# Sampled sparse attention of a decode step on one core: the order of squares, roots, score reads, top-k and tails

## The reference, cut to what matters

```
s_c = einsum('blghd,bcgd->bghlc', qg, kc) * scale + bias_c     # scores of the 64 compressed blocks
p_c = masked_softmax(s_c, dist_c >= 0);  o_cmp = p_c @ vc
ps = sum over heads of p_c, pairs of blocks added              # 32 blocks of 64 keys, and the block of the new ones
score = where(forced, 1e4, ps);  top_val, top_idx = top_k(score, 16)
ks = rms_norm(rows[:, :, 2], g_k[1])                           # every cached key is normalised
o_sel = masked_softmax(q @ ks[top blocks] * scale + bias) @ vs[top blocks]
kw = rms_norm(win_k, g_k[2]);  o_win = softmax over the window @ win_v
o = gate0 * o_cmp + gate1 * o_sel + gate2 * o_win
```

## Time and profile before

| | us |
|---|---|
| median of 3 runs | 3475.95 (3474.07 to 3480.38) |
| the profiled execution: its time | 3476.59 |
| the profiled execution: its span | 3474.7 |
| PE busy | 3191.6 (92%) |
| DVE busy | 1594.4 (46%) |
| ACT busy | 1274.2 (37%) |
| POOL busy | 204.1 (6%) |
| sampled sparse attention (from 811 to 1054 us of the span) | 243 |
| PE busy in it | 153.0 |

### The profile page before, as it was taken

How to read it: one execution, slowest core, us unless ns; L and a number is a source line. 1 busy time by engine, 2 the same in 40 slices (tenths; PEclk the granted TensorE clock), 3 DMA queues, 4 the chain that set the end, 5 groups by cost and what they waited for, 6 DMA issues and landing times. The chain is left out here.

```text
span 3474.7 us, 56585 instructions
## 1 busy us (share of the span) xinstructions
PE 3191.6 (92%) x23855; PEld 2983.6 (86%) x23855; DVE 1594.4 (46%) x1672; ACT 1274.2 (37%) x1312; POOL 204.1 (6%) x137
## 2 busy tenths in 40 slices
PE   7899999875669999999999999967789999999999
PEld 6799999753338999999999999945389999999999
DVE  5543444345554544334443354355755443344433
ACT  5432344334553434323333342235034343233332
POOL 0000000012330000000000000025200000000000
PEclk9999999978889999999999999977799999999999
DMA  6555454414554445455555545303644554555553
GB/s 217 155 166 176 140 165 127 158 49 134 183 170 165 150 158 169 159 169 167 162 169 164 166 147 167 121 33 105 242 133 144 167 167 161 169 163 164 169 161 134
DMA packets 317268, 537.10 MB, mean 155 GB/s; under 512 B 18245, under 2 KB 115519, under 8 KB 316104
## 3 DMA queue, kind: packets, MB, share of 16 engines
q1 hardware_dynamic: 316440, 529.73, 47.3%
q10 hardware_dynamic: 624, 4.46, 0.3%
HBM read 517.23 MB, written 25.19 MB: 156 GB/s over the span
## 5 line engine op out<-in xcount | busy, mean ns | idle before, releaser
L509 DVE TENSOR_TENSOR project_weights_low<-ring,project_weights_high 128x2048 fp32r<-128x2048 f32 x344 | 788.4, 2292 | 1207.1 <-ACT project_weights_high L441 1207.1
L441 ACT ACTIVATE project_weights_high<-ring 128x2048 fp32r<-128x2048 f32 x344 | 658.7, 1915 | 1256.7 <-PE project_banks L369 1256.6
L367 PE MATMUL project_banks<-high,project_weights_high 128*128 128x288 f32 x2560 | 762.0, 298 | 31.2 <-DVE project_weights_low L499 27.3
L368 PE MATMUL project_banks<-low,project_weights_high 128*128 128x288 f32 x2560 | 760.4, 297 | 0.0
L369 PE MATMUL project_banks<-high,project_weights_low 128*128 128x288 f32 x2560 | 760.1, 297 | 0.0
L367 PE MATMUL project_banks<-up_high,project_weights_high 128*128 128x288 f32 x2048 | 605.7, 296 | 0.0
L368 PE MATMUL project_banks<-up_low,project_weights_high 128*128 128x288 f32 x2048 | 605.5, 296 | 0.0
L369 PE MATMUL project_banks<-up_high,project_weights_low 128*128 128x288 f32 x2048 | 605.3, 296 | 0.0
L367 PEld LDWEIGHTS project_banks<-high,project_weights_high 128*128 128x128 f32 x2560 | 487.1, 190 | 32.9 <-DVE project_weights_low L499 28.1
L368 PEld LDWEIGHTS project_banks<-low,project_weights_high 128*128 128x128 f32 x2560 | 486.7, 190 | 0.0
L369 PEld LDWEIGHTS project_banks<-high,project_weights_low 128*128 128x128 f32 x2560 | 485.5, 190 | 0.0
(11 more groups left out here) (516 smaller groups left out, 3033.3 us busy)
## 6 DMA issues: line engine op xcount, KB each, us to landing
ring<-in_w_up_dram SPq DMA_DIRECT2D x128, 1024.0 KB, 5.3
ring<-in_w_down_dram SPq DMA_DIRECT2D x128, 1024.0 KB, 5.1
ring<-in_gla_w_in_dram SPq DMA_DIRECT2D x40, 1024.0 KB, 5.1
h<-in_cache_nsa_kv_dram SPq DMA_DIRECT2D x256, 128.0 KB, 2.3
ring<-in_w_out_dram SPq DMA_DIRECT2D x32, 1024.0 KB, 5.2
ring<-in_nsa_w_in_dram SPq DMA_DIRECT2D x28, 1024.0 KB, 5.1
sp_keys_values<-in_cache_nsa_kv_dram SPq DMA_DIRECT2D x80, 256.0 KB, 3.8
ring<-in_w_mem_kv_dram SPq DMA_DIRECT2D x16, 1024.0 KB, 5.3
```

What stands on the lines that cost most here:

```text
L367: nc.tensor.matmul(bank, w_high, moving_high[:, kt], start=(kt == 0), stop=False)
L368: nc.tensor.matmul(bank, w_high, moving_low[:, kt], start=False, stop=False)
L441: nc.scalar.activation(weights_high[:, c % 2], g.ring[:, c % RING], ACT.Copy).then_inc(rounded, 1)
L509: nc.vector.tensor_tensor(weights_low[:, c % 2], g.ring[:, c % RING], weights_high[:, c % 2].bitcast(F32), ALU.subtract).then_inc(split, 1)
```

## The change

The change gives other places to the same instructions. On ACT, a tick is now `square(k+2)`, `root(k+1)`, `copy_keys(k)`. On DVE, `sum_squares(k+2)` comes ahead of `take_scores`, which moves from even to odd ticks. The top-k is cut by pair: pair 0's stays in the front, those of pairs 1, 2 and 3 go to ticks 3.5, 5.5 and 7.5, each with its own bias instructions (three small ones for each pair in place of three for all). Tails move by one tick for the sets and the output, and by half a tick for DVE's scaling. The front of ACT and PE moves as well: ACT's exponential goes behind `square(0)`, PE's group sum behind `turn_keys(0)`.

```
 tensor:  front   yield -0.5 -> 0.5;  yield 1.5 -> 2.5
          tails   tail(t, 2) -> 3;  2.4 + 0.4 * i -> 3.4 + 0.4 * i;  tail(t, 5) -> 6
 scalar:  tails   2 + 0.4 * i -> 3 + 0.4 * i   (copy_set);  tail(t, 1.2) of the exponential stays
 vector:  front   yield 0.1 -> 0.6
          tails   tail(t, 1.6) -> 2.1;  4.9 -> 5.9;  5.5 -> 6.5   (tail(t, 1.1) stays)
@@ scalar
             def front():
+                yield -1.5
                 act.wait_ge(cmp_shifted, 1)
                 nc.scalar.activation(s_cmp[:], s_cmp[:], ACT.Exp).then_inc(cmp_exped, 1)
-                yield 1.5
+                yield 2.5
...
                     yield k
+                    if in_range(k + 2):
+                        square(k + 2)
                     if in_range(k + 1):
                         root(k + 1)
                     if in_range(k):
                         copy_keys(k)
-                    if in_range(k + 2):
-                        square(k + 2)
@@ vector
                 for t in range(PAIRS):
+                    if t:
+                        yield 2 * t + 1.5
                     for r in range(TOP_ROUNDS):
...
-                linked(nc.vector.tensor_scalar(unselected[:], block_score[:], 0.0, MASKED, ALU.is_ge, ALU.mult))
...
+                    linked(nc.vector.tensor_scalar(unselected[:, t], block_score[:, t], 0.0, MASKED, ALU.is_ge,
+                                                   ALU.mult))
+                    linked(nc.vector.tensor_scalar(sel_bias[:, t], unselected[:, t], far, None, ALU.add))
...
                         invert(k + 1)
-                    if k % 2 == 0 and in_range(k - 1):
-                        take_scores((k - 2) // 2)
                     if in_range(k + 2):
                         sum_squares(k + 2)
+                    if k % 2 and in_range(k - 2):
+                        take_scores((k - 3) // 2)
```

More of the change, by code:

```diff
@@ L1950, in front @@
                 mm.then_inc(small_scored, 1)
-                yield -0.5
+                yield 0.5
                 pe.wait_ge(cmp_ready, 1)
@@ L2028, in tails @@
                 for t in range(PAIRS):
-                    yield tail(t, 2)
+                    yield tail(t, 3)
                     pe.wait_ge(scaled, t + 1)
@@ L2033, in tails @@
                     for i in range(SETS):
-                        yield tail(t, 2.4 + 0.4 * i)
+                        yield tail(t, 3.4 + 0.4 * i)
                         multiply_set(t, i)
@@ L2037, in tails @@
                             turn_set(t, i + 2)
-                    yield tail(t, 5)
+                    yield tail(t, 6)
                     pe.wait_ge(o_taken, t + 1)
@@ L2104, in tails @@
                     for i in range(SETS):
-                        yield tail(t, 2 + 0.4 * i)
+                        yield tail(t, 3 + 0.4 * i)
                         copy_set(t, i)
@@ L2164, in front @@
                 linked(nc.vector.memset(block_score[:, :, half - 1:half + 1], FORCED))
+                near = g.bias_near[:, 0:P].rearrange("p (n k) -> p n k", k=SEL_LEN)
                 for t in range(PAIRS):
+                    if t:
+                        yield 2 * t + 1.5
                     for r in range(TOP_ROUNDS):
@@ L2171, in front @@
                         linked(nc.vector.match_replace(block_score[:, t], top[:, r], block_score[:, t], MASKED))
[L2173 to L2179, removed]
+                    linked(nc.vector.tensor_scalar(unselected[:, t], block_score[:, t], 0.0, MASKED, ALU.is_ge,
+                                                   ALU.mult))
+                    linked(nc.vector.tensor_scalar(sel_bias[:, t], unselected[:, t], far, None, ALU.add))
+                    linked(nc.vector.tensor_tensor(
+                        near_bias[:, t].rearrange("p (n k) -> p n k", k=SEL_LEN), near,
+                        unselected[:, t, half - 2:half].unsqueeze(2).to_broadcast([P, 2, SEL_LEN]), ALU.add))
             def sum_squares(n):
@@ L2237, in tails @@
                                             ).then_inc(negated, 1)
-                    yield tail(t, 1.6)
+                    yield tail(t, 2.1)
                     dve.wait_ge(exped, t * 2 + 2)
```

17 lines of the change are left out of this document (8 added, 9 removed).

## The result

The changed kernel takes 3471.14 us in the median (20 runs, 3465.36 to 3476.07), the kernel before 3478.14 in the same session (20 runs). The ratio is 0.9979, 95% interval 0.9973 to 0.9985: 7 us faster, where the forecast had 12.9. The forecast of 3463 us was made from a kernel before at 3475.95, its median of 3 runs. The profiled execution took 3470.92 us with a span of 3469.1, so 5.7 less than the one before.

The account below looks back on a forecast made before the run. It took the stage as bound by waits in one loop through ACT and DVE, with loads binding next. Terms 78.2 + 51.1 + 51.1 + 45.4 = 225.8 against 238.7, 12.9 us less, gave a median of 3463 us, range 3450 to 3473.

Parts of the forecast that it names:

- SP's loads of halves 16, 26 and 36: SP queue, loads released by set 1 of a pair: to start near 892, 943 and 994 in the profile after.
- A steady half: Loop through ACT and DVE: engines could do a half in 2.4 to 3.0 us, against 3.8 before.
- L0 to L16: Stage from the start of half 0's load to half 16's: 78.2 us for 87.2, bounds 74.5 and 82.
- three of its four parts now go to ticks 3.5, 5.5 and 7.5, where DVE has room: DVE's top-k in the first halves: the moved pieces, with 2 us of added small instructions, are hidden there.
- L10: Start of half 10's load on SP: forecast at 852.7, 38.7 us after the start of half 0's load.
- L16 to L36: Two stretches, from half 16's load to half 26's and on to half 36's: 51.1 us each, for 53.0 and 52.2.
- Free of waits, SP starts half 33: SP's loads after a release: half 33 starts 22.7 us after half 26, 3.2 us a half.
- The cost of the scaling at nothing: DVE's later scaling in the tails: costs nothing, covered by TensorE's turn and score of 3.9 us; uncovered 0 to 1.9 a tail.
- L36 to the end: From half 36's load to the next stage's first load: 45.4 us for 46.3, bounds 44 and 47.
- The rival that the pace does not change: Steady halves: copies wait for turns, a half stays at 3.8 us, time 3476, no change; chance 0.15.
- The loads: Rival at SP's loads after the releases: crowded DMA queues make the kernel slower, 3488 at 1.2 us more each; chance 0.09.
- The full gain: Rival: the loop's gain comes through with high clock in the tails, 24 us less, 3452, down to 3446; chance 0.18.

Follow-up runs that it names:

- e10: Changed kernel with the top-k pieces of pairs 1, 2 and 3 moved behind the joined maxima of the pair before: 3469.02 us, ratio to before 0.9977.
- e1: Changed kernel with the small TENSOR_SCALAR of each sum of squares gone from DVE, ACT's root taking both as scale and bias: 3469.89 us, ratio to before 0.9976.
- e13: Changed kernel, compressed probabilities turned one tick later and copied two later, top-k pieces of pairs 1 to 3 behind the joined maxima: 3468.03 us, ratio to before 0.9966.
- e16: Changed kernel with only DVE's scaling back at step 1.6, ahead of the invert; the sets stay a tick later: 3470.25 us, ratio to before 0.9979.
- e12: Changed kernel with sets and outputs of the tails at their old places, DVE's scaling left late at step 2.1: 3469.34 us, ratio to before 0.9978.
- e6: Kernel before with only ACT's tick as square, root, copies and DVE's sum ahead of the score read on odd ticks: 3455.04 us, ratio to before 0.9933.

## Why the prediction was right or wrong

**Direction and loop: right.** The copies left the loop and the roots' waits fell under 20 us (10.6). SP's loads of halves 16, 26 and 36 came at 894, 946 and 997, for 892, 943 and 994; counted from L0, which was 1.8 us earlier, they were 3.6 to 4.7 later than the sum has them. ACT stood for DMA at their squares 6 to 7 us, not 3 to 5. A steady half takes 3.2 us, for 2.72 worked out and 2.4 to 3.0 as its range. It had been 4.4 and not 3.8: the prediction read the pace from a tick without a score read.

**L0 to L16: the step that failed.** It is "three of its four parts now go to ticks 3.5, 5.5 and 7.5, where DVE has room", and with it the halves followed "one by one with the durations above". 78.2 was forecast, 81.8 came; L10 alone was 4.3 late. DVE had no room: with a piece two halves take it 7.9 us, 3.95 a half where I gave it 2.4, and the pieces delay L10 by 1.8 (e10). Taking the small instruction away (e1) hardly moves L10, because half 3 is still turned at 29.4. ACT's copy of the compressed probabilities, which the prediction did not price at all, and the piece ahead of half 6 are the two moves that give L10 back 3.6 of 4.3 at the same low clock (e13). The 1.7 us by which half 3 was late (turned 29.7 after L0, for 28) go with TensorE's clock: with 0.71 for 0.61 it is turned at 28.0 (e16). These shares overlap, so they are not to be added. Behind L10 the terms are 0.9 too short up to the end of the exponential and 1.5 too long from there to the release.

**L16 to L36: the sum right, 51.1 and 51.1 for 52.1 and 51.2, but its terms not; that is luck.** The terms from L26, forecast and measured, are: up to the square of half 33 28.2 and 31.1, from there to the end of the exponential 9.3 and 8.1, to turn_keys(33) 5.0 and 4.8, to the release 8.6 and 7.1. From L16 the first term is 32.1 and the others are the same. The first failed at "Free of waits, SP starts half 33 [...] 22.7 us after half 26". Loads of halves 30 and 33, then the square of half 33:

```profile
959.33 6.38 SPq L1916 DMA_DIRECT2D sp_keys_values<-in_cache_nsa_kv_dram  x8
...
971.36 5.76 SPq L1916 DMA_DIRECT2D sp_keys_values<-in_cache_nsa_kv_dram  x8
```

```profile
977.30 1.06 ACT L2052 ACTIVATE mem_v<-sp_keys_values 128x1024 f32<-128x1024 f32 x1 [0.98 <-DMA sp_keys_values<-in_cache_nsa_kv_dram]
```

Half 33 was issued 25.2 us after half 26. The load of half 30 waited for turn_keys(25), which ran at 957.23, because its root stood behind the blocked square of half 26 until 952.57. Before, half 30 was issued 11.2 us after half 26 and now 13.2. The last term fell short of its forecast because the clock rose earlier: score and sets in the tail of pair 2 ran partly at the high one (score 1.68, sets 0 and 1 0.83, for 1.92 and 1.29 in the tail of pair 0).

The cost of the scaling at nothing held in this kernel (e16), and so did turn and score at low clock, 3.9 (1.97 and 1.92 in the tail above). The range for a scaling without cover, 0 to 1.9 a tail, was too small: e12 gives 4.7. The prediction weighed the wait for POOL at the scaling and not at the small instruction, where it came. What the sum did not show is how much the tails take: it set their loss inside each term. With the old tails (e6) the same two stretches are 47.2 and 46.6.

**L36 to the end: mis-sized, 48.4 for 45.4.** Half 37 was to be squared 9.1 us after L36 and was at 12.0: issued 4.5 after half 36, not 3.6, and landed in 7.4, not 5.5. turn_keys(39) came at 25.2, not 23.3. The last tail took 1 us more from the scaling on; both windows run from there to the end of the stage, changed kernel and then the one before:

```profile
1032.90:1045.70 12.80, 12.68 (x206) 9.24 (x206) 0.04 (x1) 3.36 (x6) 0.00 (x0) 0.68 0.01 3
```

```profile
1041.00:1052.70 11.70, 11.64 (x206) 8.47 (x206) 0.00 (x0) 3.36 (x6) 0.00 (x0) 0.75 0.02 3
```

The same 206 matmuls ran at a granted clock of 0.68 in the mean for 0.75 (a mixture of its two levels, 1.2 and 2.4 GHz), after the same pause of 7.4 us. Why it rose later isn't settled.

**The rivals.** The rival that the pace does not change (0.15) fell: a half went from 4.4 to 3.2. Its square of half 33 at 32.0 nearly came (31.1 and 32.1), but by the late load of half 30. The loads (0.09) did not make it slower, though seven halves cost 2.5 us more than the 22.7. The full gain (0.18) was to come by a high clock in the tails, which came only in part; e6 shows a gain of 23 us with a tail as slow as before (8.7 us from the end of the exponential to the release of half 16, for 8.6): what stood against it were the tails' own places. In the chances, 0.55 and 0.18 are 0.73, and less a little can't be the 0.74 that stands there.

## What to carry to other kernels

When one change reorders a loop and moves what releases the next loads, price the two apart: here the new tick brought 23 us and the later tails took 14 of them, and a forecast of the sum alone looked like a fair gain. Work that frees a buffer belongs ahead of the loop's next step on every engine it passes; moving it back on one engine cost as much here as on both. Before an instruction is removed from an engine that looks critical, look what else the next step waits for: here the small instruction went (e1), and half 10 was loaded at the same time. And check a sum term by term, since a right total can hide two wrong terms.

## What the runs showed of the hardware

A DVE instruction on 128x8 numbers that takes 0.17 us alone ended within 0.03 us of the end of POOL's multiplication of SBUF tiles whenever that had begun first: 0.88 us in 39 of the 40 halves of the changed kernel, 0.57 where it began later beside POOL (e6, half 16). The form with a scalar and the one with two tensors did so alike; the reduction of 128x1024 beside the same POOL instruction took 1.17 us and was not held up. In the kernel before, the copy of 32 columns of the earlier trace rows met POOL instead, and its longest, 1.66 us from 872.01, ended at 873.67, 0.04 after POOL: the new order moved that wait from the copy to the small instruction. The removal of the small instruction changed the time of the changed kernel by less than the runs can tell.

The same instructions met a different TensorE clock in different executions: 0.61 and 0.71 in the same 16 us of two kernels whose programs are alike up to there, and the halves behind were 1.7 us earlier at the higher one, up to L10.
